# Router logits by token, merge gates loaded ahead of modulation weights, differential outputs scaled once a tile

## The chip, the cores and the metric

One Trainium2 chip, one of its cores. The metric is the device time of one execution of the whole program in microseconds, lower is better. The engines are called as in the profile: PE is TensorE's matmuls and PEld its weight loads, DVE is VectorE, ACT is ScalarE, POOL is GpSimd, SP is SyncE, which here only issues transfers. Each engine runs its own instructions in order and waits on semaphores for the others.

## The reference

Two layers of a decoder on 512 tokens of 1024 features, float32. Cut to what this change touches:

```python
h = modulate(rmsnorm(x, norm_mix[l]), sh1, sc1); proj = h @ w_in[l]
# differential attention, 4 heads, blocks of 128 queries
p1 = causal_probs(q1, k1); p2 = causal_probs(q2, k2)      # two softmaxes
o = einsum('bhqk,bkhd->bqhd', p1 - lam * p2, v)
o = rmsnorm(o, o_g) * (1.0 - lam_init)
# merge of the four mixers
branch = einsum('bsnw,nwd->bsnd', ys, w_branch[l])
gate = sigmoid(gates.reshape(B, S, N_BRANCH, D))
x = x + gt1[:, None, :] * (sum(gate * branch, axis=2) @ w_out[l])
# experts, 16 of them, two per token
h2 = modulate(rmsnorm(x, norm_ffn[l]), sh2, sc2)
scores = sigmoid(einsum('bsd,de->bse', h2, router_w))
```

The shifts, scales and gates (`sh1` to `gt2`) are six sections of `silu(c) @ ada_w[l]`, the modulation.

## The kernel before, in words

Every engine's program is written out by hand, one function per engine (`block.sync`, `block.tensor`, `block.scalar`, `block.vector`, `block.gpsimd`), and the two layers are unrolled. Nothing is scheduled by a program: the order of the lines is the order on each engine. The wide products run as three matmuls of rounded operands (`three`, high times high, high times low, low times high). ACT makes the high part of each weight block (L1587) and DVE the low part (L2106) in a ring of four 1 MB slots, `ring`, and two buffers for the high parts, `WH`.

**The differential sweep.** `sweep(DIFF)` goes through 16 units, one per block of 128 queries and head. For unit n, PE computes two score tiles into banks 6 and 7 and then works at gate products; DVE takes the row maxima (`rowmax`), ACT the exponentials with their sums (L1732, sums in `dl`), and DVE combines the two probability tiles in `combine`: reciprocals of the sums (L2359), the second times minus lambda (L2361), the first tile scaled by the first reciprocal (L2364), the second tile scaled and added (L2366). PE waits for that in `turn_probs` (its transposes, L872), then multiplies by the values. After every fourth unit `tile_out` copies a bank of 128x512 to `y_tok` (L2375). The sliding-window sweep does its copy with a multiply by a reciprocal that is spread over the head (L2386).

**The merge.** Eight blocks of work, q = 0 to 7 (two halves g of the output features, four mixers br). For each, PE makes four products of 512 columns into three PSUM banks in turn (`MERGE_BANKS`), so the fourth product needs the bank of the first. DVE empties each by a multiply with the gate (L2711, L2716), ACT has turned the gate logits into gates (L1940), and POOL adds to the sum (L3058). The gate logits lie in DRAM. `merge_gate(q)` loads 1 MB of them on SP into one of two buffers, `DVt` for even q and `SQKV` for odd (L625). The weights of the block come by `load(("branch", q))` (L636). Beside this DVE computes one section and then another of the modulation in four portions, `ada_late(i)`, during q = 1, 2, 4 and 5, from `ada_w` that SP loads with `late(i)` (L708), 2 MB each, even i to `TM`, odd i to `DQK`. DVE signals the end of each q by `gates_used` (the memset, L2733), and PE signals `stage_done` when the last mixer's outputs have been transposed, midway in q = 1; until then `DQK` holds them.

**The router.** After the output product and the second norm, H holds the features in rows and the tokens in columns, and ACT hands over its eight blocks of 128 features one after the other (L1687, `h_ready`). PE runs five warming matmuls (`warm(5, 5)`: they write bank 5 and nobody reads them) and then the router product with `rw` as the stationary operand: 16 experts by 512 tokens, eight products. ACT takes the sigmoid of that (L1970). PE transposes it back to tokens in rows, in four small transposes to bank 7, between the first and the second tile of `token_rows`, which turns H itself to tokens in rows for the gather, 8 transposes for each of four tiles, each copied by ACT (L1976). ACT copies the turned scores (L1981), and DVE starts on the selection of experts (L2766 onwards). PE goes on with `warm(9, 5)` and then the counting matmuls, for which it needs DVE's choice.

A float32 matmul that isn't rounded shows in the trace as two PE instructions, so 8 products are x16 and one warming matmul is x2.

## Time and profile before

| | us |
|---|---|
| median of 3 runs | 2244.61 |
| lowest and highest | 2240.77, 2245.73 |
| the profiled execution, its own time | 2246.07 |
| its span in the trace | 2244.3 |
| mean granted TensorE clock | 0.986 of full |
| PE busy | 2129.4 (95%) |
| DVE busy | 1483.5 (66%) |
| ACT busy | 1010.8 (45%) |
| matmuls in the chain that ended last | 76% |

The share of busy PE is modelled from pipelined matmuls, so that gaps below 0.2 us between them don't show. Times in the rows below are from the start of the span. A bracket behind an instruction of a timeline is how long its engine sat idle before it and which engine and line ended that.

### The profile page before, as it was taken

What the parts mean: (1) busy time and instruction counts of PE and PEld (TensorE: products, weight loads), DVE (VectorE), ACT (ScalarE), POOL (GpSimd) and SP (SyncE); (2) the same over time, 40 slices, a digit from 0 to 9 for tenths busy, and PEclk for the clock granted to TensorE, in tenths of its full rate; (3) what the DMA queues carried; (4) which work ended last, traced back from release to release, by engine and by line L of the source; (5) the groups of instructions that cost most, each with busy time, mean ns of one, the idle gap of its engine ahead of it and who ended that gap; (6) DMA issues with size and microseconds to landing.
All of it is one profiled execution on the core that took longest, in us unless ns stands there. A gap on an engine that the chain in (4) does not pass through costs nothing.

```text
span 2244.3 us, 32746 instructions
## 1 busy us (share of the span) xinstructions
PE 2129.4 (95%) x12051; PEld 1707.2 (76%) x12051; DVE 1483.5 (66%) x2695; ACT 1010.8 (45%) x1867; POOL 377.3 (17%) x346
## 2 busy tenths in 40 slices
PE   8999999999899999999999999999998989999996
PEld 5897788787687786777679978888966878777774
DVE  4737766655767876777646477666467688377775
ACT  4523334554565324555435333345445644445551
POOL 2002200000001431354300021000000024124441
PEclk9999999999999999999999999999999999999998
DMA  9332233241325665766642223333222267546653
GB/s 313 94 88 62 81 118 94 76 120 57 91 91 199 242 240 211 277 253 244 193 150 88 81 81 91 102 112 96 78 69 80 87 234 269 203 165 241 244 210 120
DMA packets 196573, 333.71 MB, mean 149 GB/s; under 512 B 30528, under 2 KB 153280, under 8 KB 180416
## 3 DMA queue, kind: packets, MB, share of 16 engines
q1 hardware_dynamic: 169184, 305.33, 40.1%
q0 software_dynamic: 19296, 19.98, 2.8%
q10 hardware_dynamic: 7936, 6.30, 0.9%
q8 instruction: 99, 1.62, 0.3%
q14 instruction: 58, 0.48, 0.1%
HBM read 352.48 MB, written 51.38 MB: 180 GB/s over the span
## 4 chain that ended last, share of the span: by engine, by line
PE 75%; DVE 11%; ACT 5%; issue 3%; DMA 3%; POOL 0%; SPq 0%; POOLq 0%; DVEq 0%; ACTq 0%
PE ps L874 70%; PE ps L872 6%; DVE spare L2088 2%; DVE ring_rounded L2106 2%; ACT WH_rounded L1587 2%; DMA SQKV<-gate_logits 1%; DMA DVt<-gate_logits 1%; DVE nmax L2343 1%; DMA Y<-y_rows 1%; DVE SC L2716 0%; DVE ps L2340 0%; DVE ssq L2273 0%; POOL M L3058 0%; DVE SC L2366 0%; DVE SQKV L2284 0%
## 5 line engine op out<-in xcount | busy, mean ns | idle before, releaser
L874 PE MATMUL ps<-X_rounded,WH_rounded 128*128 128x512 f32 x768 | 341.0, 444 | 15.9 <-DVE ring_rounded L2106 4.5
L2106 DVE TENSOR_TENSOR ring_rounded<-ring,WH_rounded 128x512 fp32r<-128x512 f32 (+2 forms) x190 | 235.0, 1245 | 134.0 <-ACT WH_rounded L1587 133.6
L874 PE MATMUL ps<-H_rounded,WH_rounded 128*128 128x512 f32 x768 | 302.9, 394 | 8.7 <-DVE SC L2716 8.7
L874 PE MATMUL ps<-X_rounded,ring_rounded 128*128 128x512 f32 x768 | 302.6, 394 | 0.0
L874 PE MATMUL ps<-WH_rounded,X_rounded 128*128 128x256 f32 (+1 forms) x960 | 275.1, 287 | 3.1 <-ACT M L1879 1.0
L874 PE MATMUL ps<-ring_rounded,X_rounded 128*128 128x256 f32 (+1 forms) x960 | 271.6, 283 | 0.0
L874 PE MATMUL ps<-WH_rounded,H_rounded 128*128 128x256 f32 (+1 forms) x960 | 271.4, 283 | 0.0
L3058 POOL TENSOR_TENSOR M<-M,SC 128x512 f32<-128x512 f32 x48 | 75.7, 1590 | 961.4 <-DVE SC L2716 961.4
L1587 ACT ACTIVATE WH_rounded<-ring 128x512 fp32r<-128x512 f32 (+2 forms) x190 | 195.1, 1036 | 75.2 <-PE ps L874 63.1
L874 PEld LDWEIGHTS ps<-X_rounded,WH_rounded 128*128 128x128 f32 x768 | 145.5, 189 | 68.8 <-issue 27.4
L874 PEld LDWEIGHTS ps<-WH_rounded,X_rounded 128*128 128x128 f32 x960 | 184.6, 192 | 5.3 <-issue 2.4
L874 PEld LDWEIGHTS ps<-ring_rounded,X_rounded 128*128 128x128 f32 x960 | 184.6, 192 | 1.2 <-issue 1.0
L874 PEld LDWEIGHTS ps<-WH_rounded,H_rounded 128*128 128x128 f32 x960 | 184.5, 192 | 0.0
L874 PEld LDWEIGHTS ps<-H_rounded,WH_rounded 128*128 128x128 f32 x768 | 145.7, 190 | 42.2 <-issue 16.5
L874 PEld LDWEIGHTS ps<-X_rounded,ring_rounded 128*128 128x128 f32 x768 | 145.0, 189 | 32.8
L874 PE MATMUL ps<-Y_rounded,WH_rounded 128*128 128x512 f32 x384 | 151.0, 393 | 0.0
L1732 ACT ACTIVATE SC<-ps,nmax 128x256 f32<-128x256 f32 (+3 forms) x192 | 94.3, 493 | 106.1 <-DVE nmax L2343 105.5
L874 PE MATMUL ps<-Y,SC 128*128 128x64 f32 (+1 forms) x512 | 129.6, 389 | 0.0
L3042 POOL TENSOR_TENSOR Y<-M,Y 128x256 f32<-128x256 f32 x56 | 48.6, 871 | 456.6 <-ACT Y L1904 297.3
L872 PEld LDWEIGHTS ps<-ident,SC 128*128 128x128 f32 (+1 forms) x452 | 64.5, 152 | 57.3 <-issue 21.0
L874 PEld LDWEIGHTS ps<-Y,SC 128*128 128x128 f32 x512 | 76.0, 192 | 36.4 <-issue 34.8
L872 PE MATMUL ps<-ident,SC 128*128 128x128 f32 (+1 forms) x452 | 85.0, 276 | 13.4 <-DVE SC L2366 8.2
(399 smaller groups left out, 4492.1 us busy)
## 6 DMA issues: line engine op xcount, KB each, us to landing
ring<-in_w_in SPq DMA_DIRECT2D x272, 256.0 KB, 4.0
Y<-in_moe_w_down SPq DMA_DIRECT2D x18, 1024.0 KB, 6.7
ring<-in_ada_w SPq DMA_DIRECT2D x64, 256.0 KB, 4.6
ring<-in_w_branch SPq DMA_DIRECT2D x64, 256.0 KB, 5.1
TM<-in_ada_w SPq DMA_DIRECT2D x14, 1024.0 KB, 10.5
DQK<-in_ada_w SPq DMA_DIRECT2D x14, 1024.0 KB, 9.4
ring<-in_moe_w_down SPq DMA_DIRECT2D x14, 1024.0 KB, 6.2
gate_logits<-CM SPq DMA_DIRECT2D x44, 256.0 KB, 2.8
```

Of the source, the lines that this page charges most:

```text
L872: ins = nc.tensor.transpose(o, lhsT, rhs)
L874: ins = nc.tensor.matmul(o, lhsT, rhs, start=start, stop=stop)
L1587: act(high[i][:, at:at + size], ring[:, j, at:at + size], ACT.Copy).then_inc(high_ready[i], p.gives(high_ready[i], 4 if parts is None else 1))
L1732: act(probs[n % 2][i][:, 0:w], bank(b, w), ACT.Exp, bias=nmax[:, n % 2, i:i + 1], accum_out=total).then_inc((handed if s.kind == "diff" el ...
L2088: ins = v.scalar_tensor_tensor(out=part[i], in0=w[i][:, k], scalar=cact[:, k:k + 1], in1=part[i], op0=ALU.mult, op1=ALU.add)
L2106: ins = v.tensor_tensor(low[j][:, at:at + size], ring[:, j, at:at + size], high[i][:, at:at + size].bitcast(F32), ALU.subtract)
L2343: red = v.tensor_reduce(nmax[:, n % 2, i:i + 1], bank(b, w), AX, ALU.max, negate=True)
L3042: eng.tensor_tensor(half(hgQs[i], j, 1), half(hgQ[:, pr], j, 1), half(hgE[i], j, 1), ALU.mult).then_inc(qs_ready[i], p.gives(qs_ready[i]))
L3058: eng.tensor_tensor(m, m, SC[:, j], ALU.add).then_inc(added[j % 2], p.gives(added[j % 2]))
```

## The change

Three parts, in both layers.

1. The router product has H as the stationary operand and `rw` as the moving one: for each block k of features four matmuls, one for each tile of 128 tokens, of 16 columns. The result is in tokens already, in bank 6, so that the four small transposes and the copy (L1981) go away, bank 7 is not used, and ACT's sigmoid is of 128x64 in place of 16x512. Before it stands one warming matmul in place of five.
2. SP issues `late(1)` behind `merge_gate(2)` and the load of branch block 4, no longer ahead of them, and its wait for `stage_done` moves with it.
3. The differential sweep no longer scales the first probabilities. It combines p1 with minus lambda times l1/l2 times p2, and `tile_out` multiplies the output by 1/l1 with a spread over each head, in the same instruction that copied it.

```diff
@@ sync
                             alone()
                             merge_gate(1)
                             late(0)
+                        if i == 4:
                             eng.wait_ge(stage_done, p.next(stage_done))
                             alone()
                             late(1)
@@ tensor
-                warm(5, 5)
+                warm(1, 5)
                 free(6)
...
                 for k in range(NC):
                     eng.wait_ge(h_ready, p.next(h_ready))
-                    ins = mm(ps[0:NE, 6], rw[:, k], H[:, k], k == 0, k == NC - 1, last=k == NC - 1)
+                    for t in range(NT):
+                        ins = mm(ps[:, 6, t * NE:(t + 1) * NE], H[:, k, tt(t)], rw[:, k], (k, t) == (0, 0), (k, t) == (NC - 1, NT - 1),
+                                 last=k == NC - 1)
...
-                token_rows(0)
-                free(6)
-                free(7)
-                alone()
                 for t in range(NT):
-                    ins = turn(ps[:, 7, t * NE:(t + 1) * NE], scores_T[:, tt(t)], k=NE, last=t == NT - 1)
-                ins.then_inc(filled[7], p.gives(filled[7]))
-                p.mark(handed[7])
-                for t in range(1, NT):
                     token_rows(t)
@@ scalar
-                act(scores_T, ps[0:NE, 6], ACT.Sigmoid).then_inc(emptied[6], p.gives(emptied[6]))
+                act(rt[:, 0], bank(6, NT * NE), ACT.Sigmoid).then_inc(handed[6], p.gives(handed[6]))
@@ vector, combine
-                v.reciprocal(dr[:, :], dl[:, n % 2]).then_inc(vector_step, p.gives(vector_step))
+                t, h = DIFF.tile(n), DIFF.head(n)
+                v.reciprocal(dr[:, t % 2, :, h], dl[:, n % 2]).then_inc(vector_step, p.gives(vector_step))
                 eng.wait_ge(vector_step, p.given(vector_step))
-                v.tensor_tensor(dr[:, 1:2], dr[:, 1:2], neglam[:, :], ALU.mult).then_inc(
+                v.scalar_tensor_tensor(out=dratio[:, :], in0=dr[:, t % 2, 1, h:h + 1], scalar=neglam[:, 0:1],
+                                       in1=dl[:, n % 2, 0:1], op0=ALU.mult, op1=ALU.mult).then_inc(
                     vector_step, p.gives(vector_step))
                 eng.wait_ge(vector_step, p.given(vector_step))
-                v.tensor_scalar(p1, p1, dr[:, 0:1], None, ALU.mult).then_inc(vector_step, p.gives(vector_step))
-                eng.wait_ge(vector_step, p.given(vector_step))
-                v.scalar_tensor_tensor(out=p1, in0=p2, scalar=dr[:, 1:2], in1=p1,
+                v.scalar_tensor_tensor(out=p1, in0=p2, scalar=dratio[:, 0:1], in1=p1,
                                               op0=ALU.mult, op1=ALU.add).then_inc(
@@ vector, tile_out
-                    v.tensor_copy(dst, bank(b)).then_inc(handed[b], p.gives(handed[b]))
+                    v.tensor_tensor(heads(dst, DH), bank3(b, DH, DV), spread(dr[:, b, 0], DV), ALU.mult).then_inc(
+                        handed[b], p.gives(handed[b]))
```

On SP, in the merge of layer 0 (`SQKV` and `DVt` are the two gate buffers, `TM` and `DQK` the places of the modulation weights, and layer 1 reads the same):

```order
 L625 DMA SQKV<-gate_logits 128x2048
 L708 DMA TM<-in_ada_w 128x8x256 x2
-L708 DMA DQK<-in_ada_w 128x8x256 x2
-L625 DMA DVt<-gate_logits 128x2048
-L636 DMA ring<-in_w_branch 128x512 x4
+L625 DMA DVt<-gate_logits 128x2048
+L636 DMA ring<-in_w_branch 128x512 x4
+L708 DMA DQK<-in_ada_w 128x8x256 x2
 L625 DMA SQKV<-gate_logits 128x2048
 L636 DMA ring<-in_w_branch 128x512 x4
```

The two modulation loads of `late(1)` stand behind the gate load of q = 2 and the four loads of branch block 4.

On PE, at the router of layer 0, before (here a matmul is counted once, not twice as in the trace):

```order
L874 MATMUL ps<-SC,ones 128x512 x2
L874 MATMUL ps<-ones,spare 128x1 x8
L874 MATMUL ps<-lmask,ident 128x256 x5
L874 MATMUL ps<-H,rw 16x512 x8
L872 MATMUL ps<-ident,H 128x128 x8
L872 MATMUL ps<-ident,SC 128x16 x4
L872 MATMUL ps<-ident,H 128x128 x24
L874 MATMUL ps<-lmask,ident 128x256 x9
```

and now:

```order
L875 MATMUL ps<-SC,ones 128x512 x2
L875 MATMUL ps<-ones,spare 128x1 x8
L875 MATMUL ps<-lmask,ident 128x256
L875 MATMUL ps<-rw,H 128x16 x32
L873 MATMUL ps<-ident,H 128x128 x32
L875 MATMUL ps<-lmask,ident 128x256 x9
```

Eight products of 512 columns have become 32 of 16 columns, each with a weight load of its own of 128 columns, and the four small transposes are gone.

## Rows read from the trace of the kernel before

**Rows 1.** The page, section 1: busy us of each engine

```profile
PE 2129.4 (95%) x12051; PEld 1707.2 (76%) x12051; DVE 1483.5 (66%) x2695; ACT 1010.8 (45%) x1867; POOL 377.3 (17%) x346
```

**Rows 2.** PE's waits in the merge of layer 0, then of layer 1

```profile
PE ps L874 <- DVE SC L2716: 4.1, 2, 2.6
...
PE ps L874 <- DVE SC L2716: 3.8, 5, 2.6
```

**Rows 3.** Timeline of SP, merge, layer 0: start, us, line, issue

```profile
711.31 0.99 SPq L708 DMA_DIRECT2D DQK<-in_ada_w  x2
712.42 1.38 SPq L625 DMA_DIRECT2D DVt<-gate_logits  x1
```

**Rows 4.** Timeline of DVE in the merge, layer 0, then layer 1

```profile
703.18 0.06 DVE L2733 MEMSET done<- 128x1 f32 x1
...
721.52 0.06 DVE L2733 MEMSET done<- 128x1 f32 x1
725.27 0.69 DVE L2716 TENSOR_TENSOR SC<-ps,DVt 128x512 f32<-128x512 f32 x1 [3.69 <-ACT DVt L1940]
727.07 2.52 DVE L2106 TENSOR_TENSOR ring_rounded<-ring,WH_rounded 128x2048 fp32r<-128x2048 f32 x1 [1.11 <-ACT WH_rounded L1587]
...
1832.96 0.69 DVE L2716 TENSOR_TENSOR SC<-ps,DVt 128x512 f32<-128x512 f32 x1 [2.45 <-ACT DVt L1940]
1834.76 2.51 DVE L2106 TENSOR_TENSOR ring_rounded<-ring,WH_rounded 128x2048 fp32r<-128x2048 f32 x1 [1.11 <-ACT WH_rounded L1587]
```

**Rows 5.** Timeline of PE in the merge, layer 0

```profile
726.11 0.47 PE L874 MATMUL ps<-H_rounded,WH_rounded 128*128 128x512 f32 x1 [1.50 <-DVE SC L2716]
...
731.65 0.77 PE L874 MATMUL ps<-H_rounded,WH_rounded 128*128 128x512 f32 x1 [2.57 <-DVE SC L2716]
732.22 0.63 PE L874 MATMUL ps<-Y_rounded,WH_rounded 128*128 128x512 f32 x1
```

**Rows 6.** PE's waits in the differential sweep, layer 0

```profile
PE ps L872 <- DVE SC L2366: 4.1, 6, 1.2
```

**Rows 7.** DVE: the output copy; L2364, L2386 (ns min/median/max, first and last start)

```profile
L2375 DVE COPY DQK<-ps 128x512 f32<-128x512 f32 x4 | 2.8, 688 | 2.0 <-PE ps L874 2.0
...
L2364 DVE TENSOR_SCALAR SC<-SC,dr x32: 286/387/487, 528.4 to 1720.0; 128x128 f32<-128x128 f32 x8, 128x256 f32<-128x256 f32 x8, 128x384 f32<-128x384 f32 x8, 128x512 f32<-128x512 f32 x8
...
L2386 DVE TENSOR_TENSOR DQK<-ps,lrec x8: 691/691/691, 638.2 to 1794.8; 128x512 f32<-128x512 f32 x8
```

**Rows 8.** Timeline at the router: layer 0, then layer 1

```profile
840.55 4.09 PE L874 MATMUL ps<-lmask,ident 128*128 128x256 f32 x10
...
841.42 5.36 ACT L1687 ACTIVATE H<-H,mod 128x512 f32<-128x512 f32 x8 [1.02 <-DVE H L2256]
...
844.57 7.04 PE L874 MATMUL ps<-H,rw 128*16 128x512 f32 x16
...
854.25 1.15 PE L872 MATMUL ps<-ident,H 128*128 128x128 f32 x8 [0.23 <-ACT SQKV L1976]
...
855.60 1.15 PE L872 MATMUL ps<-ident,H 128*128 128x128 f32 x8 [0.20 <-ACT SQKV L1976]
...
856.58 4.05 PE L874 MATMUL ps<-lmask,ident 128*128 128x256 f32 x18
...
1949.42 7.04 PE L874 MATMUL ps<-H,rw 128*16 128x512 f32 x16 [1.03 <-ACT H L1687]
```

**Rows 9.** Chain of waits after the router, layer 0: start, us, what

```profile
856.74 5.68 PE ps L874 x34
```

**Rows 10.** Timeline of PE: small matmuls at either clock

```profile
38.14 3.14 PE L874 MATMUL ps<-ones,spare 1*128 1x1 f32 x16
...
1140.11 3.74 PE L874 MATMUL ps<-SC,ones 128*128 128x128 f32 x32
```

**Rows 11.** Windows: busy us (x) by engine, PEclk, DMA share, GB/s

```profile
38.00:40.00 2.00, 2.00 (x13) 1.99 (x13) 0.86 (x1) 0.00 (x0) 0.00 (x0) 0.66 1.07 381
40.00:42.00 2.00, 2.00 (x9) 1.90 (x9) 0.55 (x4) 0.00 (x0) 0.00 (x0) 0.50 1.05 412
```

More of the change, by code:

```diff
@@ L347, in build @@
         dl = sb("dl", 2, 2)
-        dr = sb("dr", 2)
+        dr = sb("dr", 2, 2, DH)
+        dratio = sb("dratio", 1)
         tri = sb("tri", P)
@@ L504, in build @@
         merged = M3
-        scores_T = SC[0:NE, 3]
         chunks = lambda ap: [ap[:, k * S:(k + 1) * S] for k in range(ap.shape[1] // S)]
@@ L1399, in _ @@
                     eng.wait_ge(h_ready, p.next(h_ready))
-                    ins = mm(ps[0:NE, 6], rw[:, k], H[:, k], k == 0, k == NC - 1, last=k == NC - 1)
+                    for t in range(NT):
+                        ins = mm(ps[:, 6, t * NE:(t + 1) * NE], H[:, k, tt(t)], rw[:, k], (k, t) == (0, 0), (k, t) == (NC - 1, NT - 1),
+                                 last=k == NC - 1)
                 ins.then_inc(filled[6], p.gives(filled[6]))
-                p.mark(emptied[6])
+                p.mark(handed[6])
                 def token_rows(t):
@@ L1977, in token_rows @@
                             h_copied, p.gives(h_copied))
-                token_rows(0)
-                eng.wait_ge(filled[7], p.next(filled[7]))
-                act(rt[:, 0], bank(7, NT * NE), ACT.Copy).then_inc(handed[7], p.gives(handed[7]))
-                for t in range(1, NT):
+                for t in range(NT):
                     token_rows(t)
@@ L2761, in _ @@
                 p.mark(filled[6])
-                p.mark(filled[7])
-                eng.wait_ge(handed[7], p.next(handed[7]))
+                eng.wait_ge(handed[6], p.next(handed[6]))
                 r16 = [heads(rt[:, k], NT) for k in range(6)]
```

## The prediction, made before the changed kernel had run

> **What bounds the kernel now.** I read the page's busy times first. PE is busy for 2129.4 of 2244.3 us [rows 1], so a gain must either take work from PE or close one of its waits, and a loss comes from anything that makes PE slower. Then I asked who makes PE wait in the three places of the change.
>
> In the merge, PE waits 4.1 us in two pieces in layer 0 and 3.8 us in layer 1 for the bank that DVE's multiply empties [rows 2]. DVE is late because its own work stopped: it signals the end of q = 1 at 721.52, and its first multiply of q = 2 comes 3.69 us later, released by ACT's sigmoid of the gates in `DVt`, and 1.11 us more pass before it can make the low part of the next weights [rows 4]. The sigmoid waited for a transfer which SP issued at 712.42, right behind the 2 MB of `late(1)` of 711.31 [rows 3]. So one order on SP ends in PE's wait.
>
> In the differential sweep PE waits six times, 4.1 us in all, for the combined probabilities [rows 6]. At the router PE itself is the chain: 7.04 us of router product [rows 8], then transposes, warming and counting, of which the chain of waits shows 5.68 us in one piece up to DVE's counts [rows 9].
>
> **The merge, part 2 of the change.** It removes nothing. `merge_gate(2)` and the load of block 4 move ahead of `late(1)`. `merge_gate(2)` only waits for `gates_used` of q = 0, which DVE gives at 703.18 [rows 4], so it is issued some 9 us earlier, on idle DMA engines, and the gates are there when ACT gets to them. `late(1)` is still held by `stage_done` near 711.3, and it is then alone on the queue; its data is needed by DVE only behind the first multiply of q = 2, over 10 us on. Then DVE goes from 721.52 straight on. Layer 0: 3.69 + 1.11 = 4.8 us taken from DVE's path [rows 4]. PE follows: without the 1.50 and 2.57 us waits it also escapes the slow matmuls behind the second, 0.63 and 0.77 us where the one at 726.11 takes 0.47 [rows 5]. That is 4.07 us of waits and a little more, so PE could use at least 4.1, and DVE's pace gives it 4.8. I take 4.8. Layer 1: 2.45 + 1.11 = 3.56 us of DVE idle [rows 4], and 3.8 us of PE waits [rows 2]; I take 3.6. After q = 3 everything hangs on the same signals and moves as a whole. Sum: **-8.4 us**; bounds 0 (if something else is late, below) and -9.6 (4.8 in both layers).
>
> **The sweep, part 3.** Per unit one L2364 goes, 0.29 us at 128 columns and 0.49 at 512, thus by equal steps 0.35 and 0.42 between them [rows 7]. The multiply by minus lambda, of one column, becomes a three-operand one of one column, which I price at nothing. The copy of 128x512, 0.688 us, becomes a multiply from PSUM with a spread operand, and the same form in the other sweep takes 0.691 [rows 7]: nothing. What counts is only where PE waits: six units, at widths of 256, 256, 384, 512, 512 and 512. Most of the six waits are longer than the scale; I take the instruction itself at each of the six, 2 x 0.35 + 0.42 + 3 x 0.49 = 2.6, and round down to 2.5 us a layer, since the shortest waits can't give all of it. Elsewhere PE has gate products to do and the shorter DVE path is hidden by them. Sum for two layers: **-5.0 us**; bounds -2 and -8 (all the waits).
>
> **The router, part 1.** It removes 8 x 2 PE instructions, 7.04 us [rows 8], four small transposes that lie in PE's waits for ACT's copies (0.23 us of idle time even behind the second tile [rows 8]), ACT's copy, and four of the five warming matmuls, whose ten instructions took 4.09 us. It adds 32 matmuls, 64 instructions. A matmul with a full 128-column weight load doesn't get cheaper with fewer columns: 32 of them with 128 columns take 3.74 us, 0.117 each [rows 10]. So 64 cost at least 7.5 us at full clock, against 7.04. No PE time is saved even then.
>
> In layer 0 the old product could not start before 844.57, because the warming ran at half clock [rows 8]. ACT's eight instructions of 5.36 us from 841.42 on make the first block ready at 842.1 [rows 8], so the new one starts 2.5 us earlier and could end at 849.6 in place of 851.6: -2.0. In layer 1 it starts with the first block at 1949.42 as before, and ends 0.5 us later. DVE's selection starts earlier by the transposes and the copy, but behind the router the chain is PE's [rows 9], and 18 warming instructions of 4.05 us stand in it [rows 8], so this is hidden. With a full clock the router is worth -2.0 + 0.5 = -1.5 us.
>
> But I don't expect a full clock. Near the start of the program PE runs 32 instructions of one column, one behind the other. PE is busy 2.00 of 2.00 us in 38:40 and in 40:42, and yet the granted clock is 0.66 as a mean of 38:40 and 0.50 in 40:42 [rows 11]: it went from 2.4 to 1.2 GHz with PE busy throughout. The 16 instructions that straddle this take 3.14 us [rows 10]; if 4 of them ran at 0.117, the other 12 took 0.22 each. The router by token is such a stream, 16 columns behind each load of 128, twice as long. At 0.22, 64 take 14.1 us. Layer 0 enters it at the low clock already, as the old warming did: 842.1 + 14.1 = 856.2 against 851.6, +4.6. Layer 1 enters at the full clock, and I give it 10 at 0.117, a guess, since the trace shows no such stream of that length: 1.2 + 54 x 0.22 = 13.1 against 7.04, +6.0. Behind it the first tiles of transposes still run at the low clock: 8 x 0.22 = 1.76 us a tile against the 1.35 us from one tile's start to the next's now, 854.25 to 855.60 [rows 8]; two tiles, +0.8 each layer. Sum: **+12.2 us**; bounds -1.5 and +15 (0.22 throughout in both, and all four tiles slow).
>
> The Trainium skill speaks against this step of mine: "TensorE: Matmul & The Clock Gate", section "What's actually happening", has the gate follow how busy PE has recently been, and calls the low state idle. Read plainly, a gapless stream of loads and matmuls would keep 2.4 GHz, and the sum would be -14.9 in place of -1.2. The row of 38:40 disagrees with that plain reading.
>
> **Sum.** -8.4 - 5.0 + 12.2 = -1.2 us against the profiled execution's own 2246.07 (span 2244.30, and 1.8 around it). The median is 1.5 below that execution, so I put the forecast on the median: 2244.6 - 1.2 = **2243.4 us**, no change that can be told. A measurement of this kernel tells some 0.2%, 4.5 us.
>
> **Rivals.**
> - *The clock holds in the router.* For it: its stream has no gap, and 16 columns are more than one. The Trainium skill's rule above would give this. Against: the same loads in 38:40. Time: 2244.6 - 8.4 - 5.0 - 1.5 = 2229.7. It also has a half way, one layer holding or the clock falling late, at -5 to -10. Chance 0.25 together.
> - *The low clock outlasts the router.* If the transposes do not bring the clock back, the four tiles cost 4 x 0.41 = 1.6 us more, and the 18 warming instructions 0.41 us each, as the ten of 4.09 us, in place of 4.05 / 18 = 0.225, +3.3 [rows 8]. That is +4.9 a layer where I have 0.8, so -1.2 + 8.2 = +7.0, 2251.6, slower. It decides when more than three of the four tiles are still slow. Against it: transposes of 128 columns, with waits between them, give the full clock in this very place now: the next 18 instructions run at 0.225. Chance 0.12.
> - *The merge gains nothing:* `late(1)` becomes what is late. If its 2 MB came more than 10 us behind their issue, DVE would stand at its first portion in q = 2 as long as it stands for the gates now; all 8.4 us go, 2244.6 - 1.2 + 8.4 = 2251.8. Against it: nothing else is on the queue then. Chance 0.06.
> - *The change doesn't do what it says:* SP's queue could hold `merge_gate(2)` back. The order of SP shows nothing between `late(0)` and it but `gates_used`. Chance 0.02, with the last one's time.
>
> **How the numbers follow.** The forecast has 0.55; its own range is the sum with the router between +8 and +15 and the merge and sweep within 2, 2237 to 2248. Of that 0.12 lies below 2240.1, 0.40 within 0.2%, 0.03 above. Faster: 0.25 + 0.12 = 0.37. Same: 0.40 and a little of the third rival, 0.43. Slower: 0.03 + 0.12 + 0.05 = 0.20. The range of 8 in 10 takes in the rival at 2229.7 and leaves out the two near 2252: 2229 to 2250.
>
> **What would show it.** Right: in the merge, DVE's wait for ACT at its first multiply of q = 2 gone in both layers, and PE's waits behind L2716 below 1 us each; L2364 gone and PE's waits for the combined probabilities down from 4.1 to some 1.6 us; in the windows of the router a granted clock of 0.50, and the 64 instructions taking 11 to 14 us. Wrong: these 64 in about 7.5 us at 1.00, which makes it the first rival; the 18 warming instructions behind the tiles taking over 6 us, the second; or DVE's portion of the modulation waiting for its weights in q = 2, the third.

## The result, and the profile after

| | before | after |
|---|---|---|
| median, us (20 runs each, taken together) | 2245.68 | 2249.12 |
| lowest and highest | 2240.77, 2250.43 | 2243.42, 2253.12 |
| the profiled execution, its own time | 2246.07 | 2251.32 |
| its span | 2244.3 | 2249.6 |
| mean granted TensorE clock | 0.986 | 0.978 |

The ratio is 1.0016, with an interval of 1.0009 to 1.0023: slower by 3.6 us (2.0 to 5.2). Not the -1.2 of the forecast, and on the other side of zero; at 0.16% it is less than the 0.2% that I had called no change, and more than this larger number of runs leaves uncertain.

The page after, section 1. It answers to [rows 1]: PE is busy for 13.0 us more, in a span that is 5.3 us longer.

```profile
PE 2142.4 (95%) x12123; PEld 1731.4 (77%) x12123; DVE 1474.5 (66%) x2663; ACT 1010.7 (45%) x1865; POOL 381.7 (17%) x346
```

**The router.** Timeline of PE at the router of the changed kernel, layer 0 and then layer 1. It answers to [rows 8].

```profile
838.58 0.68 PE L875 MATMUL ps<-lmask,ident 128*128 128x256 f32 x2
840.22 13.19 PE L875 MATMUL ps<-rw,H 128*128 128x16 f32 x64 [0.96 <-ACT H L1682]
853.25 6.58 PE L873 MATMUL ps<-ident,H 128*128 128x128 f32 x32
859.67 4.05 PE L875 MATMUL ps<-lmask,ident 128*128 128x256 f32 x18
...
1943.93 0.59 PE L875 MATMUL ps<-lmask,ident 128*128 128x256 f32 x2
1947.27 13.83 PE L875 MATMUL ps<-rw,H 128*128 128x16 f32 x64 [2.75 <-ACT H L1682]
1960.95 6.14 PE L873 MATMUL ps<-ident,H 128*128 128x128 f32 x32
1966.92 4.05 PE L875 MATMUL ps<-lmask,ident 128*128 128x256 f32 x18
```

In both layers the 64 instructions take over 13 us, 0.206 and 0.216 each, against 7.04 for the 16 that they replace. The 18 warming instructions behind take 4.05 us, as before: by then the clock is back. In layer 1 it came back while the 32 transposes ran, as two windows show. Columns: stretch, its length, busy us (and instructions) of PE, PEld, DVE, ACT, POOL, then PEclk, DMA share, GB/s.

```profile
1962.00:1964.00 2.00, 2.00 (x11) 1.62 (x10) 1.69 (x10) 1.32 (x3) 0.00 (x0) 0.51 0.98 410
1964.00:1966.00 2.00, 1.73 (x13) 1.12 (x12) 1.69 (x10) 1.81 (x4) 0.00 (x0) 1.00 0.87 352
```

What I had not seen coming stands in the timeline above, in the second row of layer 1: PE sat idle for 2.75 us ahead of the router. Before, five warming matmuls filled that time up to 1.03 us. The windows, with the same columns, show what that did.

```profile
1943.00:1945.00 2.00, 1.52 (x4) 0.64 (x4) 0.00 (x0) 0.84 (x2) 0.00 (x0) 1.00 0.00 0
1945.00:1947.00 2.00, 0.00 (x0) 0.00 (x0) 1.45 (x3) 0.98 (x2) 0.00 (x0) 0.97 0.00 0
1947.00:1949.00 2.00, 1.73 (x9) 1.73 (x9) 2.00 (x4) 2.00 (x4) 0.00 (x0) 0.50 0.21 29
1949.00:1951.00 2.00, 2.00 (x11) 2.00 (x11) 2.00 (x4) 2.00 (x4) 0.00 (x0) 0.50 0.87 283
```

The clock is 0.50 from the first instruction of the router on, not after ten of them. (In layer 0 it is 1.00 in the stretch from 838 to 840, before the router, and falls within the stretch from 840 to 842, with the router under way, to a mean of 0.74 and then 0.50.)

**The merge.** Timeline of DVE and then POOL in q = 2, layer 0, after. It answers to [rows 4].

```profile
723.62 0.68 DVE L2709 TENSOR_TENSOR SC<-ps,DVt 128x512 f32<-128x512 f32 x1
723.63 0.06 DVE L2726 MEMSET done<- 128x1 f32 x1
724.22 2.27 DVE L2098 TENSOR_TENSOR ring_rounded<-ring,WH_rounded 128x2048 fp32r<-128x2048 f32 x1
726.42 1.64 DVE L2083 TENSOR_SCALAR spare<-DQK,cact 128x256 f32<-128x256 f32 x2
...
724.48 3.17 POOL L3050 TENSOR_TENSOR M<-M,SC 128x512 f32<-128x512 f32 x1 [1.86 <-DVE SC L2709]
```

The two waits of 3.69 and 1.11 us are gone: the multiply starts with the end of q = 1 and the low part of the weights directly behind it. But L2083, two instructions, takes 1.64 us where it took 0.60, and POOL's sum 3.17 where it took 1.29 in the same place of the trace before (timeline of POOL):

```profile
726.14 1.29 POOL L3058 TENSOR_TENSOR M<-M,SC 128x512 f32<-128x512 f32 x1 [5.65 <-DVE SC L2716]
```

L2083 by instruction (ns of one: min/median/max), first the changed kernel, then the one before:

```profile
L2083 DVE TENSOR_SCALAR spare<-DQK,cact x10: 337/342/1376, 726.4 to 1870.1; 128x256 f32<-128x256 f32 x10
```

```profile
L2091 DVE TENSOR_SCALAR spare<-DQK,cact x10: 340/342/349, 729.5 to 1872.3; 128x256 f32<-128x256 f32 x10
```

One of the two took 1.38 us instead of 0.34. PE's waits for L2709 in the merge are down to 1.7 us in layer 0 and 1.6 in layer 1, four pieces each, from 4.1 and 3.8 [rows 2]:

```profile
PE ps L875 <- DVE SC L2709: 1.7, 4, 0.6
...
PE ps L875 <- DVE SC L2709: 1.6, 4, 0.6
```

**The sweep.** L2364 is gone, and PE's wait for the combined probabilities in layer 0 has halved, from 4.1 us in six pieces [rows 6]:

```profile
PE ps L873 <- DVE SC L2358: 2.0, 4, 0.7
```

**A place that nobody changed.** Windows of the first product of the merge, layer 0, in the trace after and then in the one before, with the same columns as above:

```profile
688.00:690.00 2.00, 1.86 (x5) 1.51 (x6) 1.80 (x3) 1.99 (x2) 0.00 (x0) 0.50 0.92 280
690.00:692.00 2.00, 2.00 (x6) 1.61 (x5) 0.64 (x2) 2.00 (x4) 0.00 (x0) 0.50 1.02 343
692.00:694.00 2.00, 2.00 (x7) 1.51 (x7) 2.00 (x5) 2.00 (x3) 0.00 (x0) 0.50 0.97 371
```

```profile
688.00:690.00 2.00, 1.51 (x7) 1.29 (x8) 2.00 (x4) 1.99 (x2) 0.00 (x0) 1.00 0.76 236
690.00:692.00 2.00, 2.00 (x13) 1.65 (x11) 0.43 (x2) 2.00 (x3) 0.00 (x0) 1.00 1.10 367
692.00:694.00 2.00, 2.00 (x10) 1.66 (x9) 2.00 (x4) 2.00 (x4) 0.00 (x0) 1.00 0.93 343
```

The instructions are the same, and PE makes 18 of them in these 6 us instead of 30, at a clock of 0.50 instead of 1.00. The stretch from 520 to 524 us, also unchanged code, is at 0.57 in the trace after and at 1.00 in the one before.

**The time by stages.** I took the starts of the same DVE instructions in both traces and subtracted. What a stage costs is by how much this difference grows within it. The same in a second execution of the changed kernel (after_again, below), and in a second execution of the one before, all against the first trace of before:

| stage | after | after_again | before_again |
|---|---|---|---|
| layer 0 up to the sweep | +2.0 | -0.2 | +1.1 |
| differential sweep, layer 0 | **-2.4** | **-2.4** | +0.1 |
| start of the merge (698 to 703) | +2.5 | +1.2 | 0.0 |
| merge, q = 2 to 7, layer 0 | **-4.1** | **-4.1** | 0.0 |
| router to DVE's counts, layer 0 | **+5.0** | **+5.3** | 0.0 |
| on to the sweep of layer 1 | -0.9 | +0.7 | -0.2 |
| differential sweep, layer 1 | **-2.5** | **-2.4** | 0.0 |
| start of the merge, layer 1 | +0.4 | +0.4 | 0.0 |
| merge, q = 2, layer 1 | **-2.9** | **-2.9** | 0.0 |
| on to the router of layer 1 | +0.7 | +0.6 | 0.0 |
| router to DVE's counts, layer 1 | **+7.5** | **+7.6** | 0.0 |
| to the end | -0.2 | +0.1 | +1.2 |
| whole, to DVE's last instructions | +5.2 | +3.8 | +2.1 |

Between these two executions the changed stages (bold) repeat within 0.3 us, and they give +0.6 and +1.1. Everything else is the same code, and still differs: by up to 2.5 us a stage in the changed kernel, by up to 1.2 in the one before.

### The profile page after: what moved, and what is told of

It reads as the page before. It is cut to its first block, busy times and chain, and to the rows that moved or that the text cites. A ratio compares the mean times of both kernels' runs of the same rounds, so it can differ in the third digit from the quotient of the medians.

```text
span 2249.6 us, 32852 instructions
## 1 busy us (share of the span) xinstructions
PE 2142.4 (95%) x12123; PEld 1731.4 (77%) x12123; DVE 1474.5 (66%) x2663; ACT 1010.7 (45%) x1865; POOL 381.7 (17%) x346
## 4 chain that ended last, share of the span: by engine, by line
PE 76%; DVE 11%; ACT 5%; issue 3%; DMA 2%; POOL 0%; SPq 0%; POOLq 0%; DVEq 0%; ACTq 0%
PE ps L875 71%; PE ps L873 6%; DVE spare L2080 3%; DVE ring_rounded L2098 2%; ACT WH_rounded L1582 1%; DMA SQKV<-gate_logits 1%; DVE nmax L2335 1%; DVE SC L2709 1%; DMA Y<-y_rows 1%; DVE ps L2332 0%; DVE ssq L2265 0%; POOL M L3050 0%; DVE spare L2083 0%; DVE H L2248 0%; DVE SQKV L2276 0%
## 5 line engine op out<-in xcount | busy, mean ns | idle before, releaser
L873 PEld LDWEIGHTS ps<-ident,SC 128*128 128x128 f32 x444 | 63.7, 152 | 50.9 <-issue 20.7
L875 PE MATMUL ps<-Y 64*128 64x64 f32 (+2 forms) x976 | 91.1, 296 | 5.4 <-issue 4.4
```

What stands on the lines that cost most here:

```text
L873: ins = nc.tensor.transpose(o, lhsT, rhs)
L875: ins = nc.tensor.matmul(o, lhsT, rhs, start=start, stop=stop)
```

## The experiments

All kernels are made from the one before or the changed one. The ratios are to runs of the kernel before on the same chip. The three parts of the change are meant as numbered ahead of the diff.

### One part at a time, and two without the router

```diff
@@ merge_alone: the kernel before, sync
+                        if i == 4:
                             eng.wait_ge(stage_done, p.next(stage_done))
                             alone()
                             late(1)
@@ sweep_alone: the kernel before, vector: all hunks of combine and tile_out, and no other
@@ router_alone: the kernel before, tensor, scalar and vector: all hunks of the router
@@ no_router: the changed kernel with the hunks of the router taken back
```

> The kernel before with part 2 alone: late(1) issued behind the gates of q = 2 and block 4. The prediction has -8.4 us; the two traces of before and after put the gain at 4.2 us in layer 0 and 2.6 in layer 1, so my present theory is -6.8, ratio 0.997. Rival, that late(1) becomes what is late: 0 or above, with DVE waiting for the modulation weights in q = 2.

> The kernel before with part 3 alone: the first softmax's sum applied once a tile. The prediction has -5.0 us for two layers, ratio 0.9978. PE's waits for the combined probabilities in layer 0 should fall from 4.1 to about 2.0 us as in the changed kernel. Rival, that the gate products covered most of it: -1 to -3.

> The kernel before with part 1 alone: router product by token, one warming matmul in place of five. The theory that the low clock makes its price: the 64 instructions take 13 to 14 us in both layers at a granted clock of 0.50, and the time is +14 (prediction +12.2), ratio 1.006. Rival, that the loss of the whole change lay elsewhere, in stages that differ from one execution to the next: +5 or less.

> The change without part 1, that is parts 2 and 3 on the router as it was. If the parts add up, this is the sum of merge_alone and sweep_alone, -11 to -13 us, ratio 0.9945, and faster than both kernels. Rival, that parts 2 and 3 gain on the same waits or are given back later: less than -8.

| kernel | median, us | ratio, interval | from the ratio, us |
|---|---|---|---|
| merge_alone | 2239.42 | 0.9975 (0.9966 to 0.9984) | -5.6 |
| sweep_alone | 2243.67 | 0.9991 (0.9982 to 1.0000) | -2.0 |
| router_alone | 2259.23 | 1.0068 (1.0055 to 1.0082) | +15.3 |
| no_router | 2233.79 | 0.9952 (0.9938 to 0.9965) | -10.8 |

(Kernel before in these runs: 2245.79.) The first result is the sign of each part: two gain, one loses more than both. The sweep's -2.0 (-4.0 to 0.0) is nearer to its rival of -1 to -3 than to the -5.0 of the prediction. Taking the router back from the change turns +3.6 into -10.8 and beats both kernels. The sum of the three single ratios is +7.7 and the whole is +3.6; with intervals of 2 to 3 us on each either side this is no contradiction, but it doesn't give the parts to a microsecond. In the traces the stages of the parts are sharper: merge -4.0 and -2.9 in merge_alone, -4.1 and -2.9 in no_router; sweep -2.4 and -2.4 in no_router, with the same 2.0 us of waits of PE in layer 0 in both kernels that have part 3. In sweep_alone the sweep of layer 0 gains the same 2.4, but 1.4 us are lost directly behind it (618 to 624), and layer 1 gains 1.1, with a loss of 1.3 in its midst (at 1631). The router is +7.5 in layer 1 in router_alone, the same as in the change, but only +3.4 in layer 0. There its 64 instructions took 11.44 us, not the expected 13 to 14: they began at 842.72, and the clock fell only between 844 and 846 (0.85 as a mean of these two us, 0.50 behind).

### The router's loss: warming, columns, or the number of instructions

```diff
@@ warm1_alone: the kernel before, tensor
-                warm(5, 5)
+                warm(1, 5)
@@ warm5_by_token: the changed kernel, tensor
-                warm(1, 5)
+                warm(5, 5)
@@ held: warm5_by_token, and behind the four products of each block k
+                    if k < NC - 1:
+                        mm(bank(5, 2 * P), ident[:, :], flat(lmask[:, 0:2]))
@@ split_before: the kernel before, tensor
-                    ins = mm(ps[0:NE, 6], rw[:, k], H[:, k], k == 0, k == NC - 1, last=k == NC - 1)
+                    for t in range(NT):
+                        ins = mm(ps[0:NE, 6, tt(t)], rw[:, k], H[:, k, tt(t)], (k, t) == (0, 0), (k, t) == (NC - 1, NT - 1),
+                                 last=k == NC - 1)
```

> The kernel before with one warming matmul in place of five, and nothing else. In layer 1 of the changed kernel PE stood 2.75 us before the router and entered it at a clock of 0.50. If the missing warming matmuls are what lowered it, this kernel shows it too: the 16 router instructions of layer 1 partly at half speed, 9 to 12 us in place of 7.04, and +2 to +5 us in all; in layer 0 they start earlier, which gives up to 2.5 back. Rival, that the warming is worthless: 0 to -2.5.

> The changed kernel with its five warming matmuls back. If the stream of loads with 16 columns lowers the clock by itself, the 64 instructions of layer 1 start at 1.00 and fall to 0.50 within a few us, about 12 to 13 us in place of 13.8, and the whole stays within 2 us of the changed kernel, +2 to +4 against the kernel before. Rival, that the clock was lost only because PE stood idle before: the 64 take about 7.5 us at 1.00 in layer 1, and the whole is -3 or better against the kernel before.

> The changed kernel with five warming matmuls, and one matmul of 256 columns that nobody reads behind each of the first seven blocks of the router product, 14 instructions more. If the clock is what costs, and wide work holds it, the stream runs at 1.00: 64 x 0.117 + 14 x 0.225 = 10.6 us in layer 1, less than the 13.8 without them though it is more work, and the whole is about -3 us against the kernel before. Rival, that a load of 128 columns with 16 behind it costs 0.21 us whatever the clock: 13.8 + 3.2 = 17 us, and the whole is +7 or more.

> The kernel before with its eight router products of 512 columns cut into 32 of 128 columns, rw still stationary, 64 instructions as in the changed kernel. It tells the number of instructions from the number of columns. If columns hold the clock, the granted clock stays at 1.00 and the 64 take 7 to 8 us, no change against the kernel before (within 2 us). Rival, that 64 short instructions with a load each cost the clock or 0.2 us each: 13 us, +5 to +7 a layer.

| kernel | median, us | ratio, interval |
|---|---|---|
| warm1_alone | 2246.34 | 1.0005 (0.9993 to 1.0018) |
| warm5_by_token | 2246.23 | 1.0002 (0.9990 to 1.0014) |
| held | 2251.09 | 1.0032 (1.0013 to 1.0050) |
| split_before | 2247.67 | 1.0010 (0.9999 to 1.0022) |

(Kernel before: 2245.99.) split_before first: 64 instructions as in the change, but 128 columns behind a load of 16. Timeline of PE, layer 1, and one window:

```profile
1949.26 7.16 PE L874 MATMUL ps<-H,rw 128*16 128x128 f32 x64 [1.02 <-ACT H L1689]
...
1953.00:1955.00 2.00, 2.00 (x21) 1.78 (x19) 0.09 (x1) 1.98 (x3) 0.00 (x0) 1.00 1.02 430
```

7.16 us at 1.00, against 7.04 for the 16 wide ones, and the same 7.16 in layer 0. So neither the number of instructions nor the writing in pieces costs more than 0.12 us a layer, and the rival falls. (The whole came to +2.2 us, -0.2 to +4.9, of which the router stages have 0.2.) This kernel changed two things against the stream by token, though: more moving columns and a narrower load. That the load of 128 isn't what keeps the clock down is seen in the transposes shown above: they load 128 columns too, with 128 moving ones, and the clock rises from 0.51 to 1.00 while they run.

warm5_by_token has the stream of 16 columns with the warming that it had before. Timeline of PE, layer 1, and windows:

```profile
1940.15 12.14 PE L875 MATMUL ps<-rw,H 128*128 128x16 f32 x64 [1.02 <-ACT H L1682]
...
1940.00:1942.00 2.00, 1.84 (x17) 1.85 (x17) 2.00 (x5) 2.00 (x4) 0.00 (x0) 1.00 1.00 418
1942.00:1944.00 2.00, 2.00 (x12) 2.00 (x12) 1.99 (x3) 2.00 (x4) 0.00 (x0) 0.51 1.02 430
1944.00:1946.00 2.00, 2.00 (x11) 2.00 (x11) 0.00 (x0) 1.98 (x3) 0.00 (x0) 0.50 1.00 422
```

Here the stream starts at 1.00 and falls to 0.50 within two us, with PE busy 2.00 of 2.00: the stream itself lowers the clock, as [rows 11] had shown for one column. In layer 0 PE doesn't even pause before it. Timeline of PE and windows there:

```profile
833.93 2.40 PE L875 MATMUL ps<-lmask,ident 128*128 128x256 f32 x10
836.17 10.59 PE L875 MATMUL ps<-rw,H 128*128 128x16 f32 x64
...
836.00:838.00 2.00, 2.00 (x20) 1.97 (x18) 2.00 (x5) 2.00 (x4) 0.00 (x0) 1.00 0.85 303
838.00:840.00 2.00, 2.00 (x19) 2.00 (x18) 1.48 (x4) 2.00 (x4) 0.00 (x0) 0.89 0.95 385
840.00:842.00 2.00, 2.00 (x11) 2.00 (x11) 0.00 (x0) 1.44 (x2) 0.00 (x0) 0.50 1.02 430
```

So no pause is needed for the fall. The stream took 12.14 us in layer 1, in the expected 12 to 13, and 10.59 in layer 0. The whole came to +0.4 us (-2.2 to +3.1), below the expected +2 to +4, and below the change by 3.1 with an uncertainty of about the same size. The stages are clearer: 2.4 us less than in the change in layer 0 and 1.4 in layer 1. Four warming matmuls more, and less time.

warm1_alone shows the other half. Timeline of PE, layer 1:

```profile
1945.01 8.74 PE L874 MATMUL ps<-H,rw 128*16 128x512 f32 x16 [2.75 <-ACT H L1687]
```

The same 2.75 us of idle time, and then the old product takes 8.74 us in place of 7.04, a little less than the expected 9 to 12. In layer 0 DVE's counts come 1.0 us earlier; in layer 1 1.7 later. As a whole it can't be told from no change (+1.1, -1.6 to +4.0), where +2 to +5 was expected.

held has 14 instructions more in the stream, and in its first profile the shorter one. Timeline of PE in layer 1, the first two blocks; then the same in a second execution, held_again:

```profile
1937.78 1.06 PE L875 MATMUL ps<-rw,H 128*128 128x16 f32 x8 [1.02 <-ACT H L1684]
1938.70 0.68 PE L875 MATMUL ps<-lmask,ident 128*128 128x256 f32 x2
1939.21 0.96 PE L875 MATMUL ps<-rw,H 128*128 128x16 f32 x8
1940.02 0.68 PE L875 MATMUL ps<-lmask,ident 128*128 128x256 f32 x2
```

```profile
1936.52 1.06 PE L875 MATMUL ps<-rw,H 128*128 128x16 f32 x8 [1.02 <-ACT H L1684]
1937.43 0.68 PE L875 MATMUL ps<-lmask,ident 128*128 128x256 f32 x2
1937.94 0.96 PE L875 MATMUL ps<-rw,H 128*128 128x16 f32 x8
1938.76 1.13 PE L875 MATMUL ps<-lmask,ident 128*128 128x256 f32 x2
1939.68 1.73 PE L875 MATMUL ps<-rw,H 128*128 128x16 f32 x8
```

In the first execution all 64 run at 0.12 us each, as 8 in 0.96, and the 78 instructions need 10.2 us in layer 0 and 10.3 in layer 1: at the full clock a load of 128 columns with 16 behind it costs what [rows 10] said. In the second the clock falls at 1938.76 and stays down: blocks of 1.73 and wide ones of 1.20, 17.5 us from the first block to the tiles. My bet on the mechanism was right, the bet on the remedy wrong: the median is +7.2, and its twelve times go from 2237.30 to 2262.90, with clocks from 0.990 to 0.977. With wide matmuls between the narrow ones the clock stays at 1.00 in some executions and not in others.

### Chance in the unchanged stages, and a further try

before_again and after_again are the two kernels once more, held_again is held once more, one profiled execution each. best_try is no_router with one warming matmul in layer 0 only:

```diff
-                warm(5, 5)
+                warm(1 if l == 0 else 5, 5)
```

> The kernel before, a second time. If the stages without a change differ between executions by where PE's pauses fall in the clock's course, this trace differs from the first by 1 to 2.5 us in places of its own (around 300 to 340, 400, 520, 690 to 703, 1510), and its clock by up to 0.003. Rival, that each kernel has a fixed pattern: within 0.3 us of the first trace everywhere.

> The changed kernel, a second time. The changed stages repeat: sweep -2.4 a layer against before, merge -4.1 and -2.9 (DVE's 1.4 us long L2083 and POOL's 3.2 us long sum in q = 2 again), router +5 and +8 to +9. The 2.5 us that the first trace lost at the start of the merge of layer 0, with PE at a clock of 0.50 from 688 to 694, come from chance, and are not there in about every second execution; if the change itself makes them, they are there again.

> The router by token with a matmul of 256 columns behind each block, a second time. The first profile is its fastest execution (2237.3) and shows 1.00 through both routers; its median is 2251.1. My theory: the clock is held only in some executions, and this one shows at least one router at 0.50 for most of its 78 instructions, 18 to 20 us in place of 10.2. Rival, that the router always holds and the 14 us come from elsewhere: both routers at 10.2 us again.

> Parts 2 and 3 on the router as it was, and in layer 0 one warming matmul in place of five (layer 1 keeps five). In warm1_alone the router of layer 0 came 1.9 us earlier than with five, and that of layer 1 lost 2.9 by the same edit. So -1.9 against no_router, about 2232, ratio to the kernel before 0.9945 or lower. Rival, that the low clock eats it up: as no_router, 2234.

The table by stages above has the first two. The changed stages repeated; the start of the merge lost 1.2 us instead of 2.5. before_again differed from before by +1.1 and +1.2 us in two stages and by next to nothing in the others, so differences in unchanged stages belong to the kernel before as well. held_again lost its clock in the router of layer 1 (17.5 us) and kept it in that of layer 0 up to the last block. best_try: 2235.40 us, ratio 0.9945 (0.9932 to 0.9959), not to be told from no_router's 0.9952. The router of layer 0 takes 1.0 us less in its trace than in the kernel before, as it does in warm1_alone (the expectation took 1.9 for that, which was too much).

But against no_router, from which it is made, it is no gain at all: there the same stage takes 1.7 us less than in the kernel before. Timeline of PE in layer 0, no_router and then best_try:

```profile
835.52 2.40 PE L876 MATMUL ps<-lmask,ident 128*128 128x256 f32 x10
837.86 7.04 PE L876 MATMUL ps<-H,rw 128*16 128x512 f32 x16
...
834.42 0.68 PE L876 MATMUL ps<-lmask,ident 128*128 128x256 f32 x2
836.06 8.44 PE L876 MATMUL ps<-H,rw 128*16 128x512 f32 x16 [0.96 <-ACT H L1689]
```

The five warming matmuls of layer 0 took 4.09 us in the kernel before [rows 8], with a clock of 0.50 from 842 to 844, and 2.40 here, at 1.00. It doesn't look like a matter of the execution: they take 2.40 us in all five traces that have five of them and part 2 of the change (merge_alone, no_router, warm5_by_token, held, held_again), and 4.05 to 4.61 in all four that have five and lack part 2 (before, before_again, split_before, sweep_alone). So in the traces part 2 is worth another 1.7 us at a place that it doesn't touch, as long as the five stand there. That PE comes to that place some microseconds earlier goes with it; why the clock then stays up, no run shows.

### All eight combinations

```diff
@@ merge_router: the changed kernel with the hunks of combine and tile_out taken back
@@ sweep_router: the changed kernel with the hunk of sync taken back
```

> Parts 1 and 2 without the sweep's part 3. With it and the next kernel all eight combinations of the three parts are measured, and each part's worth is a mean of four differences. By the stages of the traces: merge -7.0, router +12.7, so +5.7, ratio 1.0025. By the single medians (merge -5.6, router +15.3): +9.7, ratio 1.0043. The stages: merge -4.1 and -2.9, router +5.1 and +7.6 up to DVE's counts.

> Parts 1 and 3 without the merge's part 2. By the stages of the traces: sweep -4.9, router +12.7, so +7.8, ratio 1.0035. By the single medians (sweep -2.0, router +15.3): +13.3, ratio 1.006. If the sweep's gain is given back systematically at the start of the merge, where PE then comes earlier, the trace shows +1.2 or +2.5 us there; if by chance, anything from 0 to 2.5.

merge_router: 2251.97 us, 1.0033 (1.0021 to 1.0045), +7.4, between the two expected values of +5.7 and +9.7. sweep_router: 2255.81 us, 1.0051 (1.0037 to 1.0064), +11.5, between +7.8 and +13.3. (Kernel before: 2245.14.) Now each part has four differences, from the ratios of pairs that differ by it alone, in us:

| part | alone | with one | with the other | with both | mean | by stages | forecast |
|---|---|---|---|---|---|---|---|
| merge | -5.6 | -8.8 (sweep) | -7.9 (router) | -7.9 | **-7.5** | -7.0 | -8.4 |
| sweep | -2.0 | -5.2 (merge) | -3.8 (router) | -3.8 | **-3.7** | -4.9 | -5.0 |
| router | +15.3 | +13.0 (merge) | +13.5 (sweep) | +14.4 | **+14.0** | +12.6 | +12.2 |

With single intervals of 2 to 3 us either side, a mean of four is good to about 2 us, so the means and the stages agree. The question that I had left open, whether the sweep's gain is given back at the start of the merge by rule, is answered by sweep_router: it comes 4.6 us early there and loses nothing between 698 and 703, where the change lost 2.5 and sweep_alone 1.2. best_try and held_again, which have part 3 too, lose nothing there either, and merge_alone, which has no part 3, lost 1.2. sweep_router lost 1.5 us elsewhere, at 618 to 624, as sweep_alone did; so did split_before, without part 3.

## Why the prediction was wrong

**The steps that held.** PE bounds the kernel; both gains were real, and both came from PE's waits. The sweep: forecast -2.5 a layer, measured -2.4 and -2.5 by stages, and the waits fell from 4.1 to 2.0 us (I had 1.6). The low clock under a gapless stream: forecast 0.22 us an instruction from the row of 38.14, measured 0.206 to 0.216 in the change. The rival of the clock that holds, with its chance of 0.25, fell: 13.19 and 13.83 us for the 64, not 7.5. The Trainium skill's rule that spoke for it ("TensorE: Matmul & The Clock Gate", "What's actually happening": the gate follows how busy PE has recently been) doesn't hold here if read as time in which PE has work. In warm5_by_token the clock falls from 1.00 to 0.50 with PE and PEld busy 2.00 of 2.00 us. The trace disagrees with that reading. In split_before the same number of instructions, with 128 columns each, ran at 1.00. The clock came back with the transposes, as I had it, so the second rival fell too: the 18 warming instructions took 4.05 us.

**The term of the merge was too large.** I took 4.8 and 3.6 us, DVE's idle time, and measured 4.1 and 2.9. Both waits of DVE went, as the step says. What I left out is POOL: its sum for the first multiply of q = 2 ran before mostly in DVE's pause of 1.11 us. Now DVE has no pause. POOL's sum stretches over 3.17 us beside the low part of the weights, and then L2083 takes 1.04 us longer, 1.64 for 0.60, in both layers. That the two hold each other up was there to read in the trace of before. Timeline of DVE: four L2088 beside a sum of POOL in q = 2, and four of them in q = 4, in which POOL has nothing to add:

```profile
737.85 2.69 DVE L2088 SCALAR_TENSOR_TENSOR spare<-DQK,cact,spare 128x256 f32<-128x256 f32 x4
...
754.01 1.67 DVE L2088 SCALAR_TENSOR_TENSOR spare<-TM,cact,spare 128x256 f32<-128x256 f32 x4
```

2.69 against 1.67 us: 1.02 each time. This matches the Trainium skill ("SBUF — State Buffer", "SBUF: two separate sides"): some DVE instructions (those with two SBUF inputs, and those in a mode that uses both ports) and GpSimd's share a port pair, and whoever comes second waits for the whole instruction. So the term should have been 4.8 + 0.25 - 1.04 = 4.0, with 0.25 for the low part, 2.27 in place of 2.52 us, and in layer 1 3.56 + 0.25 - 1.04 = 2.8; measured were 4.1 and 2.9. I haven't isolated it by a kernel without that sum; it rests on these rows and on the same 1.64 us in the other kernels with part 2, where those without it have 0.60.

**The term of the router was a little too small, from errors that went against each other.** "Layer 0: +4.6" and 0.8 for tiles: 5.4, measured 5.0 to 5.3 in the change, which is in part luck. "Layer 0 enters it at the low clock already" was wrong: the clock was 1.00 just before it, and the product came to +3.8 and +4.4 in the two traces. The way from there to the counts took 1.2 and 0.9 more. "Layer 1 enters at the full clock, and I give it 10 at 0.117": it entered at 0.50. I had costed four of the five warming matmuls at nothing and even as a gain, because in layer 0 they stood ahead of the product. In layer 1 they filled PE's wait for the norm, and without them PE idled for 2.75 us and the clock was gone before the first router instruction. +6.0 became +6.8 (13.83 for 7.04 us, and no gain at the start), and the tiles and the way to the counts 0.7: +7.5 in place of +6.8. warm5_by_token says what the edit was worth: by stages +2.6 and +6.1 in place of +5.0 and +7.5, 3.8 us. In layer 0 too, then, the four matmuls earned more than they cost once the change was in.

**What turned the sign: the merge term, and a part of the sum that wasn't in it.** The measurement is +3.6 where I had -1.2, a miss of 4.8 us. By stages the three terms come to -7.0 - 4.9 + 12.6 = +0.7: all three were off toward the slow side, the merge by 1.4, the router by 0.4, the sweep by 0.1. The merge alone is enough to bring -1.2 to +0.2. The first failing step is therefore "Layer 0: 3.69 + 1.11 = 4.8 us taken from DVE's path" and its 3.6 for layer 1, -8.4 in all, by stages -7.0. It left DVE's loss beside POOL out, the 1.04 us told above, which is argued from rows and not isolated.

The other 2.9 us of the miss lie outside the three stages, and the second failing step is "**Sum**", where I took the three terms for the whole and put the rest at nothing. The 2 us either way that I gave were for the merge and the sweep, and +8 to +15 for the router, none for the unchanged stages. These moved by +4.6 us in the first trace of the change and by +2.7 in the second, but by +2.1 in the kernel before itself, and in merge_alone by -4.8 (1.7 of it is the warming of layer 0 told above). Where I compared windows, the same work ran at 1.00 in one trace and at 0.50 for a while in the other (688 to 694, 520 to 524). The price was visible in the spread of the runs, 5 us among the first three. By the means of the eight kernels the parts come to -7.5 - 3.7 + 14.0 = +2.8; these means take in what the unchanged stages do.

Whether the change shifts these stages by rule or by chance stays open. That sweep_router lost nothing where the change lost 2.5 speaks for chance at that place. But the sign does not look random: I took -7.0 us for part 2 and -4.9 for part 3 where a kernel has them, added the router stages of its own trace where its router is changed, and compared with the time by its ratio. For all eleven kernels with a ratio other than held the ratio gives more, by 0.4 us (warm1_alone) to 4.4 (router_alone), 2.3 as a mean, even in split_before (+2.0), which changes nothing but the cut of the product. Each of these differences is uncertain by 2 to 3 us, and all rest on the same kernel before, so that this is a sign and no measurement; what makes it, no run shows. The time itself, 2249.1, was at the upper end of the range of 2229 to 2250.

**The rivals on the other side.** "The merge gains nothing" fell: DVE never waited for `DQK`. That the change doesn't do what it says fell in all three parts.

## What to carry to other kernels

Price a product by what it does to PE's clock, not only by its columns: turning a stationary operand of 16 columns and a moving one of 512 into a stationary one of 128 and a moving one of 16 saved four small transposes and a copy and, together with the four warming matmuls taken away, cost 5 us in one layer and 7.5 in the other. Don't count warming matmuls as waste before knowing which pause they fill and at which clock they run. Taking four away from the kernel before gained 1.0 us in layer 0 and lost 1.7 in layer 1; with part 2 in place, the same edit lost 0.7 in layer 0 (best_try against no_router). When a change has three parts, measure them apart: here two parts were worth -10.8 us together (0.9952, 0.9938 to 0.9965), and the third turned that into +3.6.

## What the hardware showed that I had not expected

- A gapless stream of 64 instructions with a load of 128 columns and 16 moving columns brings the clock from 1.00 to 0.50 while PE counts as fully busy, with or without a pause before it; with 128 moving columns behind a load of 16 the clock stays at 1.00 (7.16 us for 64).
- A wide matmul after every eight narrow instructions gives 10.3 us in one execution and 17.5 in another, of the same kernel and place. Twelve executions spread over 25.6 us, where the kernel before spreads over 13.2 in 35.
- The five warming matmuls of layer 0, in kernels that keep them, took 2.40 us in five traces with part 2, where PE came to them some microseconds earlier, and 4.05 to 4.61 in four without.
- A pause of PE of 2.75 us in place of 1.03 cost the old product 1.7 us (8.74 against 7.04).
- POOL's sum of 128x512 and DVE's three-operand instructions hold each other up: 1.02 us of DVE for every sum of 1.3 us.
